# Four weight sums of a Winograd product: two by adding transfers and two on VectorE instead of four on GpSimd, with another product order

## The chip, the core and the metric

One of the eight cores of a Trainium2 chip runs the whole kernel. It has five engines with a queue of instructions each, which are synchronised by semaphores: TensorE (PE in the profile) multiplies, VectorE (DVE), ScalarE (ACT) and GpSimd (POOL) work element by element, SyncE (SP) starts transfers. GpSimd can start transfers too, and only its transfers may add to what lies at the destination. The metric is the device time of one execution in microseconds, less is better: 1863.03 us is the median of three runs of the kernel before (1861.79 to 1863.89).

## The reference, cut to what matters

The reference is two transformer blocks in a row on x of 512 tokens by 1024 features, in float32. The first block has two attentions and a feed-forward layer. The second has a feed-forward layer, a mixer of two attentions, and again a feed-forward layer. These last two layers are where the change lies:

```python
def swiglu(h, w1, w3, w2):
    return (jax.nn.silu(h @ w1) * (h @ w3)) @ w2

h = modulate(x, norm_g[l, 0], mod[:, 0, 0], mod[:, 0, 1])
x = x + 0.5 * mod[:, 0, 2][:, None, :] * swiglu(h, ffn1_w1[l], ffn1_w3[l], ffn1_w2[l])
```

The inputs w1 and w3 are 1024 by 2816 each, w2 is 2816 by 1024. The change also moves the computation of the rotary angles of the second block, `rope_tables(positions, ...)`: cosines and sines for the mixer that follows the first of these layers.

## The kernel before, in words

**Layout.** Activations are kept transposed, features on the 128 partitions and the 512 tokens along the row. A float32 product is done as three: every operand is split into a high part (rounded to fp32r, by ScalarE) and a low part (the rest, by VectorE), and TensorE multiplies high by high, high by low and low by high (L1438 to L1440 for 256 columns, L1451 to L1453 and L726 to L728 for 512). Weights come from memory in chunks of 128 by 1024 (512 KB) into RAW (three buffers); ScalarE makes HI from it, VectorE makes LO = RAW - HI (L2153).

**A layer by pairs.** `ffn_by_pairs` (f = 1 and 2, at about 793 and 1548 us) treats the hidden features in tiles of 128, 22 of them. The first four tiles are made plainly. The other 18 are made by pairs: pair p even is two gate tiles, pair p odd the up tiles of the same two hidden tiles. The weights of a pair are seen as a 2 by 2 block matrix: A11 and A12 (first tile, first and second half of the features) and A21 and A22 (second tile). The tokens are cut in two halves, EARLY and LATE. Winograd's form of Strassen's scheme then needs seven products instead of eight. Besides A11, A12 and A22 it multiplies four weight sums, S1 = A21 + A22, S2 = S1 - A11, S4 = A12 - S2 and S3 = A11 - A21, with token halves or sums of token halves (TH, TL; T3 and T4 are sums of their own). Each product is 12 matmuls of 256 columns (4 blocks of features, 3 split products). There are 18 pairs and so 126 products in a layer.

**Where the sums are made.** GpSimd's `sums_of` (L643 to L662) makes the four sums with tensor_tensor into SB, each after the low part of the same sum of the pair before has been made from the same place. SyncE loads the two weight tiles of a pair into SRAW[p % 3] (L595), two transfers of 512 KB, when the pair three before has been used up.

**Order of the products.** `_products` (L72) writes the order out: S1, S2, S4, A11 of the next pair, S3, A12 of the next pair, A22. Two neighbours share a chunk buffer (HI, LO); where TOGETHER holds, both halves are split by one instruction of 1024 columns, else by two of 512. `product` (L1401) lists what TensorE waits for: the low half of the weight form, and the copies or additions that free or complete a PSUM bank. A22 waits for c22_made (L1428), S4 for p5_copied (L1424).

**The loops.** TensorE, ScalarE and VectorE each walk the same list of products s. ScalarE and VectorE first finish product s - 1 (`after_product`), then split the form of product s + 4 (`ahead_hi`, `ahead_lo`), then do what was put off (`later`). VectorE adds PSUM banks to the copies (P1C, P5C, UC), multiplies the activated gate (G) by the up values (H), and makes the low part of a hidden tile (L3009). A layer has three parts a, b and c (PARTS): 30, 56 and 40 products, each followed by a down stage (`down_blocks`, L1443) in which the hidden tiles of the part are multiplied by w2 in eight blocks of 21 or 24 matmuls, into two PSUM banks in turn, and VectorE adds each block to X (L3137). At the end of parts a and b TensorE waits for the low part of the last but one hidden tile, and before the last tile of the first block for the last. In part c it does a stretch of the down product before and after the last product A22.

**Angles.** In the down stage of part c of layer f = 1 VectorE computes the rotary angles (`angles`, L2312) before the additions to X of blocks 0 and 2, and ScalarE the tables (`table`, L1759).

## Time and profile before

| what | value |
|---|---|
| median of three runs | 1863.03 us |
| the profiled execution | 1862.07 us |
| its span, first to last instruction | 1860.3 us |
| TensorE matmul busy | 1837.5 us, 99% |
| VectorE busy | 1334.8 us, 72% |
| ScalarE busy | 857.3 us, 46% |
| GpSimd busy | 270.8 us, 15% |
| mean granted TensorE clock | 0.998 |
| bytes moved, mean | 208.25 MB, 112 GB/s |

Busy time is the union of an engine's instructions, so a busy TensorE can still lose time: matmuls overlap, and a wait shorter than the overlap does not show as idle time. The span is 1.8 us shorter than the profiled execution. Rows of a timeline have the start in us, the duration in us, the engine, the line, the operation, the output and inputs, and in brackets the idle time of the engine before it with what ended it.

### The profile page before, as it was taken

What the parts mean: (1) busy time and instruction counts of PE and PEld (TensorE: products, weight loads), DVE (VectorE), ACT (ScalarE), POOL (GpSimd) and SP (SyncE); (2) the same over time, 40 slices, a digit from 0 to 9 for tenths busy, and PEclk for the clock granted to TensorE, in tenths of its full rate; (3) what the DMA queues carried; (4) which work ended last, traced back from release to release, by engine and by line L of the source; (5) the groups of instructions that cost most, each with busy time, mean ns of one, the idle gap of its engine ahead of it and who ended that gap; (6) DMA issues with size and microseconds to landing.
All of it is one profiled execution on the core that took longest, in us unless ns stands there. A gap on an engine that the chain in (4) does not pass through costs nothing.

```text
span 1860.3 us, 27681 instructions
## 1 busy us (share of the span) xinstructions
PE 1837.5 (99%) x10112; PEld 1530.2 (82%) x10112; DVE 1334.8 (72%) x2105; ACT 857.3 (46%) x1545; POOL 270.8 (15%) x248
## 2 busy tenths in 40 slices
PE   9999999999999999999999989999999999999999
PEld 7777778888888888798988968757767889899897
DVE  7778456757766666896985886866785788689394
ACT  6465445433232233452643554446655455355262
POOL 0001000001111000151532310100000103154140
PEclk9999999999999999999999999999999999999999
DMA  5211113346666563423332122211111422322213
GB/s 187 91 57 68 60 67 115 136 135 235 227 224 224 183 213 106 159 79 110 114 107 84 49 91 91 82 64 50 47 57 69 159 95 78 135 91 103 85 52 102
DMA packets 58325, 208.25 MB, mean 112 GB/s; under 512 B 6688, under 2 KB 6816, under 8 KB 58208
## 3 DMA queue, kind: packets, MB, share of 16 engines
q1 hardware_dynamic: 47232, 167.67, 26.0%
q0 software_dynamic: 10976, 39.00, 6.4%
q8 instruction: 75, 1.23, 0.3%
q14 instruction: 42, 0.34, 0.1%
HBM read 204.48 MB, written 2.10 MB: 111 GB/s over the span
## 4 chain that ended last, share of the span: by engine, by line
PE 79%; DVE 14%; issue 5%; ACT 1%; DMA 0%; SPq 0%; DVEq 0%; ACTq 0%
PE PS L726 16%; PE PS L728 15%; PE PS L727 15%; DVE LO L2962 5%; PE PS L1451 4%; PE PS L1452 4%; PE PS L1453 4%; PE PS L1223 2%; PE PS L1438 2%; PE PS L1440 2%; PE PS L1439 2%; PE PS L1263 2%; PE PS L1250 1%; DVE LO L2153 1%; DVE HL L3009 1%
## 5 line engine op out<-in xcount | busy, mean ns | idle before, releaser
L1542 ACT ACTIVATE HI<-RAW 128x1024 fp32r<-128x1024 f32 x237 | 250.5, 1058 | 326.9 <-PE PS L728 206.6
L2153 DVE TENSOR_TENSOR LO<-RAW,HI 128x1024 fp32r<-128x1024 f32 x237 | 290.7, 1227 | 131.1 <-ACT HI L1542 129.7
L726 PE MATMUL PS<-XH,HI 128*128 128x512 f32 x848 | 337.9, 398 | 0.0
L728 PE MATMUL PS<-XH,LO 128*128 128x512 f32 x848 | 330.8, 390 | 0.0
L727 PE MATMUL PS<-XL,HI 128*128 128x512 f32 x848 | 330.4, 390 | 0.0
L726 PEld LDWEIGHTS PS<-XH,HI 128*128 128x128 f32 x848 | 159.2, 188 | 39.2 <-issue 7.8
L728 PEld LDWEIGHTS PS<-XH,LO 128*128 128x128 f32 x848 | 159.2, 188 | 34.4
L727 PEld LDWEIGHTS PS<-XL,HI 128*128 128x128 f32 x848 | 159.4, 188 | 31.0
L1438 PE MATMUL PS<-TH,HI 128*128 128x256 f32 x576 | 163.8, 284 | 5.0 <-DVE Y L3037 5.0
L1439 PE MATMUL PS<-TL,HI 128*128 128x256 f32 x576 | 163.0, 283 | 0.0
L1440 PE MATMUL PS<-TH,LO 128*128 128x256 f32 x576 | 162.9, 283 | 0.0
L1451 PE MATMUL PS<-HH,HI 128*128 128x512 f32 x352 | 138.5, 393 | 5.4 <-DVE X L3137 3.7
L1452 PE MATMUL PS<-HL,HI 128*128 128x512 f32 x352 | 137.6, 391 | 0.0
L1453 PE MATMUL PS<-HH,LO 128*128 128x512 f32 x352 | 137.5, 391 | 0.0
L650 POOL TENSOR_TENSOR SB<-SRAW 128x512 f32<-128x512 f32 x36 | 48.2, 1338 | 604.0 <-DVE LO L2956 287.8
L2962 DVE TENSOR_TENSOR LO<-SRAW,HI 128x512 fp32r<-128x512 f32 x104 | 125.2, 1214 | 12.8 <-ACT HI L1644 12.8
L1438 PE MATMUL PS<-XH,HI 128*128 128x256 f32 x432 | 122.8, 284 | 1.8 <-ACT RB L1671 1.8
L1439 PE MATMUL PS<-XL,HI 128*128 128x256 f32 x432 | 122.2, 283 | 0.0
L1440 PE MATMUL PS<-XH,LO 128*128 128x256 f32 x432 | 122.2, 283 | 0.0
L1438 PEld LDWEIGHTS PS<-TH,HI 128*128 128x128 f32 x576 | 110.4, 192 | 7.2 <-DVE LO L2956 4.2
L1439 PEld LDWEIGHTS PS<-TL,HI 128*128 128x128 f32 x576 | 110.5, 192 | 0.2
L1440 PEld LDWEIGHTS PS<-TH,LO 128*128 128x128 f32 x576 | 110.5, 192 | 0.0
(478 smaller groups left out, 3853.3 us busy)
## 6 DMA issues: line engine op xcount, KB each, us to landing
RAW<-weights SPq DMA_DIRECT2D x237, 512.0 KB, 3.5
ADA<-ada POOLq DMA_DIRECT2D x72, 512.0 KB, 4.5
SRAW<-weights SPq DMA_DIRECT2D x72, 512.0 KB, 4.3
y_out<-X SPq DMA_DIRECT2D x8, 256.0 KB, 2.0
X<-x_in SPq DMA_DIRECT2D x3, 512.0 KB, 7.6
RAW<-weights SPq DMA_DIRECT2D x4, 256.0 KB, 5.5
X<-x_in SPq DMA_DIRECT2D x2, 256.0 KB, 4.5
COND<-condition POOLq DMA_DIRECT2D x1, 512.0 KB, 4.6
```

Source lines behind the costliest of these rows:

```text
L726: mm(bank, a, moving[0][:, t, :], start=start, stop=False)
L727: mm(bank, a, moving[1][:, t, :], start=False, stop=False)
L728: ins = mm(bank, z, moving[0][:, t, :], start=False, stop=stop)
L1438: mm(bank, a, xh[:, t, :], start=opens and t == 0, stop=False, skip_group_check=True)
L1439: mm(bank, a, xl[:, t, :], start=False, stop=False, skip_group_check=True)
L1440: ins = mm(bank, z, xh[:, t, :], start=False, stop=t == 3, skip_group_check=True)
L1451: mm(bank, a, hid_high(t), start=t == own[0], stop=False)
L1452: mm(bank, a, hid_low(t), start=False, stop=False)
L1453: ins = mm(bank, z, hid_high(t), start=False, stop=t == own[-1])
L1542: A(HI[n0 % 3][:], RAW[n0 % 3][:], ACT.Copy).then_inc(sem("hi_ready"), 1)
L2153: V.tensor_tensor(LO[n0 % 3][:], RAW[n0 % 3][:], HI[n0 % 3][:].bitcast(F32), ALU.subtract)\
L2962: V.tensor_tensor(half_of(LO[n % 3], h), form(kind, p), half_of(HI[n % 3], h).bitcast(F32), ALU.subtract).then_inc(sem("lo_ready" if h els ...
```

## The change

The order of products becomes S2, S1, A11 of the next pair, S3, S4, A12 of the next pair, A22. The sums have other signs: S2 = S1 + A11, S4 = S2 + A12, S3 = A21 + A11, so every sum is an addition. The missing signs go to the token forms 1, 2 and 4 (scale -1.0 in the copy and in the subtraction that makes the low part), to the silu of the second gate tile and to the products with the second up tile.

GpSimd adds nothing itself. For each pair it starts three transfers of 256 KB: A21 from memory to one of two slots in SB, A22 from memory added to A21 in SRAW, which makes S1 in place, and A11 from memory added to the slot, which makes S3. VectorE makes S2 and S4, in the iterations of S1 and S4 of the pair before. S3 and S4 share a chunk where they are neighbours; they lie side by side in SB for odd pairs. SyncE's load of a pair waits for S4 in place of S3, and its second half also for the low part of S1.

VectorE and ScalarE put their work for the hidden tiles elsewhere in their queues: the product of the first hidden tile is one instruction of 512 columns after S4, its low part is made six products after S4, the quarters of the second tile are multiplied after A22, and its low part six products later. What is left at the end of a part is done after the last product. The angles move to the down stage of part b of layer f = 1, blocks 1 and 4, and the tables one block later in part c, from buffers of their own (ANGLE). Some semaphores are merged.

```diff
@@ -73,8 +73,8 @@
-        order += [("S1", p), ("S2", p), ("S4", p)]
-        order += [("A11", p + 1)] * (p + 1 < NPAIRS) + [("S3", p)]
+        order += [("S2", p), ("S1", p)]
+        order += [("A11", p + 1)] * (p + 1 < NPAIRS) + [("S3", p), ("S4", p)]
@@ -88,7 +88,7 @@
-            PRODUCTS[2 * v][0] + PRODUCTS[2 * v + 1][0] in ("S1S2", "S2S4") for v in range(NV)]
+            PRODUCTS[2 * v][0] + PRODUCTS[2 * v + 1][0] == "S3S4" for v in range(NV)]
@@ -590,8 +601,10 @@
-                    sp.wait_ge(*form_made(f, "S3", p - 3))
+                    sp.wait_ge(*form_made(f, "S4", p - 3))
...
+                    if m:
+                        sp.wait_ge(*low_made(f, "S1", p - 3))
@@ -642,24 +655,21 @@
             def sums_of(f, p):
...
-                w = SRAW[p % 3]
-                a11, a12, a21, a22 = w[:, 0, 0:S], w[:, 0, S:2 * S], w[:, 1, 0:S], w[:, 1, S:2 * S]
+                first, second = wst[real_pair(f, p, 0)], wst[real_pair(f, p, 1)]
+                if p > 1:
+                    pool.wait_ge(*low_made(f, "S3", p - 2))
+                elif f == 2:
+                    pool.wait_ge(sem("branch_scaled"), 2 * DT)
+                else:
+                    pool.wait_ge(sem("chunk_used"), FIRST["down1"] + 3 * DT)
+                if of_pair(f, p) > 1:
+                    pool.wait_ge(sem("s3_landed"), 32 * of_pair(f, p) - 32)
+                    pool.wait_ge(sem("s1_landed"), 16 * of_pair(f, p) - 16)
+                pool.dma_start(third_sum(p), second[:, 0:S]).then_inc(sem("s3_landed"), 16)
...
-                if p:
-                    pool.wait_ge(*low_made(f, "S1", p - 1))
-                pool.tensor_tensor(SB[:, 0, :], a21, a22, ALU.add).then_inc(sem("s_made"), 1)
-                pool.wait_ge(*raw_pair(f, p, 0))
-                if p:
-                    pool.wait_ge(*low_made(f, "S2", p - 1))
-                pool.wait_ge(*form_made(f, "S1", p))
-                pool.tensor_tensor(SB[:, 1, :], SB[:, 0, :], a11, ALU.subtract).then_inc(sem("s_made"), 1)
-                if p:
-                    pool.wait_ge(*low_made(f, "S4", p - 1))
-                pool.wait_ge(*form_made(f, "S2", p))
-                pool.tensor_tensor(SB[:, 2, :], a12, SB[:, 1, :], ALU.subtract).then_inc(sem("s_made"), 1)
-                if p:
-                    pool.wait_ge(*low_made(f, "S3", p - 1))
-                pool.tensor_tensor(SB[:, 3, :], a11, a21, ALU.subtract).then_inc(sem("s_made"), 1)
+                pool.dma_start(SRAW[p % 3][:, 1, 0:S], second[:, S:2 * S], accum_op=ALU.add).then_inc(sem("s1_landed"), 16)
+                pool.wait_ge(sem("s3_landed"), 32 * of_pair(f, p) - 16)
+                pool.dma_start(third_sum(p), first[:, 0:S], accum_op=ALU.add).then_inc(sem("s3_landed"), 16)
@@ -1409,7 +1419,7 @@
                     elif kind == "A11" and p > 1 and p % 2 == 0:
...
                     elif kind == "A11" and p > 1:
-                        pe.wait_ge(sem("hid"), hid_count(f, pair_tile(p - 2, 1)))
+                        pe.wait_ge(sem("h21_made"), NPAIRS // 2 * (f - 1) + p // 2)
@@ -1676,23 +1687,32 @@
-                    A(G[1][:, EARLY], bank, ACT.Silu).then_inc(sem("part_silu"), 1)
+                    A(G[1][:, EARLY], bank, ACT.Silu, scale=-1.0).then_inc(sem("part_silu"), 1)
...
+            def silu_of_first(f, s):
...
+            def high_of_second(f, s):
+                kind, p = PRODUCTS[s]
+                if p % 2 and kind == "A22":
+                    hidden_hi(f, pair_tile(p, 1), H[1])
@@ -1722,13 +1742,18 @@
+                        if s > 2 * v0 + 3:
+                            silu_of_first(f, s - 4)
+                            high_of_second(f, s - 4)
...
-                    later(f, 2 * v1 - 1)
+                    for s in range(2 * v1 - 4, 2 * v1):
+                        silu_of_first(f, s)
+                        high_of_second(f, s)
@@ -1741,7 +1766,8 @@
-                            if m in (0, 2):
+                            if m in (1, 3):
+                                act.wait_ge(sem("hid_lo"), FT * f + FT)
@@ -3017,39 +3045,77 @@
                 if kind == "A12":
                     v.wait_ge(*product_done(f, kind, p))
...
+                    if p % 2:
+                        v.wait_ge(sem("hid_lo"), split_count(f, pair_tile(p - 2, 0)))
+                    elif p:
+                        v.wait_ge(sem("hid"), hid_count(f, pair_tile(p - 1, 0)))
...
-                    if p % 2:
-                        v.wait_ge(sem("c11_made"), of_pair(f, p))
-                        v.wait_ge(sem("part_silu"), part_silu(f, p, 1))
-                        V.tensor_tensor(H[0][:, EARLY], H[0][:, EARLY], G[0][:, EARLY], ALU.mult)
                 elif kind == "S4":
                     v.wait_ge(*product_done(f, kind, p))
...
-                        v.wait_ge(sem("part_silu"), part_silu(f, p, 2))
-                        V.tensor_tensor(H[0][:, LATE], H[0][:, LATE], G[0][:, LATE], ALU.mult)\
-                            .then_inc(sem("hid"), 1)
+                        v.wait_ge(sem("part_silu"), part_silu(f, p, 3))
+                        V.tensor_tensor(H[0], H[0], G[0], ALU.mult).then_inc(sem("hid"), 1)
                 elif kind == "S3":
                     v.wait_ge(*product_done(f, kind, p))
...
+                    if p % 2 == 0 and p:
+                        v.wait_ge(sem("hid"), hid_count(f, pair_tile(p - 1, 1)))
+                    elif p:
+                        v.wait_ge(sem("hid_lo"), split_count(f, pair_tile(p - 2, 1)))
...
-                    if p % 2:
-                        v.wait_ge(sem("c22_made"), of_pair(f, p))
-                        v.wait_ge(sem("part_silu"), part_silu(f, p, 3))
-                        V.tensor_tensor(H[1][:, LATE], H[1][:, LATE], G[1][:, LATE], ALU.mult)
                 elif kind == "A22" and p % 2:
                     v.wait_ge(*product_done(f, kind, p))
...
-                    V.tensor_tensor(H[1][:, EARLY], G[1][:, EARLY], bank, ALU.mult).then_inc(sem("hid"), 1)
-            def later(f, s):
+                    V.scalar_tensor_tensor(out=H[1][:, EARLY], in0=bank, scalar=-1.0, in1=G[1][:, EARLY],
+                                           op0=ALU.mult, op1=ALU.mult).then_inc(sem("h21_made"), 1)
+            def second_sum(f, p):
+                if p:
+                    v.wait_ge(*low_made(f, "S2", p - 1))
+                elif f == 2:
+                    v.wait_ge(sem("branch_scaled"), 2 * DT)
+                v.wait_ge(*form_made(f, "S1", p))
+                v.wait_ge(*raw_pair(f, p, 0))
+                V.tensor_tensor(form("S2", p), form("S1", p), form("A11", p), ALU.add).then_inc(sem("s_made"), 1)
+            def fourth_sum(f, p):
+                if p:
+                    v.wait_ge(*low_made(f, "S4", p - 1))
+                v.wait_ge(*form_made(f, "S2", p))
+                V.tensor_tensor(form("S4", p), form("S2", p), form("A12", p), ALU.add).then_inc(sem("s_made"), 1)
+            def sums_for(f, s):
...
-                if p % 2 and kind in ("S4", "A22"):
-                    m = int(kind == "A22")
-                    hidden_lo(f, pair_tile(p, m), H[m])
+                if kind == "S1" and p + 1 < NPAIRS:
+                    second_sum(f, p + 1)
+                elif kind == "S4" and p + 1 < NPAIRS:
+                    fourth_sum(f, p + 1)
+            def last_quarter(f, s):
+                kind, p = PRODUCTS[s]
+                if kind == "A22" and p % 2:
+                    v.wait_ge(sem("c22_made"), of_pair(f, p))
+                    V.scalar_tensor_tensor(out=H[1][:, LATE], in0=H[1][:, LATE], scalar=-1.0, in1=G[1][:, LATE],
+                                           op0=ALU.mult, op1=ALU.mult).then_inc(sem("hid"), 1)
+            def low_of_first(f, s):
+                kind, p = PRODUCTS[s]
+                if p % 2 and kind == "S4":
+                    hidden_lo(f, pair_tile(p, 0), H[0])
+            def low_of_second(f, s):
+                kind, p = PRODUCTS[s]
+                if p % 2 and kind == "A22":
+                    hidden_lo(f, pair_tile(p, 1), H[1])
@@ -3085,21 +3150,24 @@
+                second_sum(f, 0)
...
+                fourth_sum(f, 0)
...
                     for s in range(2 * v0, 2 * v1):
...
-                            if PRODUCTS[s - 1][0] == "S3":
-                                ahead_lo(v_chunk(f, (s - 1) // 2), ((s - 1) % 2,))
-                        if PRODUCTS[s][0] != "S3":
-                            ahead_lo(v_chunk(f, s // 2), (s % 2,))
-                        if s > 2 * v0 + 2:
-                            later(f, s - 3)
+                        ahead_lo(v_chunk(f, s // 2), (s % 2,))
+                        sums_for(f, s)
+                        if s > 2 * v0 + 1:
+                            last_quarter(f, s - 2)
+                        if s > 2 * v0 + 5:
+                            low_of_first(f, s - 6)
+                            low_of_second(f, s - 6)
@@ -3108,8 +3176,10 @@
-                    for s in range(2 * v1 - 3, 2 * v1):
-                        later(f, s)
+                    last_quarter(f, 2 * v1 - 1)
+                    for s in range(2 * v1 - 6, 2 * v1):
+                        low_of_first(f, s)
+                        low_of_second(f, s)
@@ -3119,12 +3189,11 @@
-                        if squares and m == 0:
+                        if part == 1 and f == 1 and m == 0:
...
-                            angles(2, POS2[:], "freq_a")
-                        if squares and m == 2:
-                            angles(3, POS2[:], "freq_i")
+                        if part == 1 and f == 1 and m in (1, 4):
+                            angles(2 + m // 4, POS2[:], ("freq_a", "freq_i")[m // 4])
```

## Rows read from the trace of the kernel before

**Rows 1.** The page: the chain that ended last, share of the span by engine.
```profile
PE 79%; DVE 14%; issue 5%; ACT 1%; DMA 0%; SPq 0%; DVEq 0%; ACTq 0%
```
**Rows 2.** Timeline of TensorE around 938 us: a wait between two products.
```profile
937.27 0.28 PE L1440 MATMUL PS<-XH,LO 128*128 128x256 f32 x1
938.00 0.36 PE L1438 MATMUL PS<-TH,HI 128*128 128x256 f32 x1 [0.46 <-DVE Y L3037]
938.20 0.28 PE L1439 MATMUL PS<-TL,HI 128*128 128x256 f32 x1
938.32 0.28 PE L1440 MATMUL PS<-TH,LO 128*128 128x256 f32 x1
```
**Rows 3.** Busy time by stretch: PE, PEld, DVE, ACT, POOL, clock, DMA, GB/s.
```profile
917.87:939.17 21.30, 20.61 (x171) 20.26 (x170) 20.91 (x25) 12.30 (x24) 11.50 (x9) 1.00 0.28 96
```
**Rows 4.** Waits of TensorE, 795 to 1062 us: total, times, longest.
```profile
PE PS L1438 <- DVE Y L3037: 2.5, 5, 0.9
PE PS L1438 <- ACT RB L1671: 0.9, 4, 0.2
```
**Rows 5.** Groups of GpSimd, 917.87 to 939.17 us: total and mean ns, idle before.
```profile
L650 POOL TENSOR_TENSOR SB<-SRAW 128x512 f32<-128x512 f32 x2 | 2.6, 1294 | 4.8 <-DVE LO L2956 2.6 <-DVE LO L2962 2.2
```
**Rows 6.** Groups of VectorE in the same stretch.
```profile
L2962 DVE TENSOR_TENSOR LO<-SRAW,HI 128x512 fp32r<-128x512 f32 x6 | 7.7, 1298 | 0.3 <-ACT HI L1644 0.3
L2962 DVE TENSOR_TENSOR LO<-SB,HI 128x512 fp32r<-128x512 f32 x4 | 3.8, 961 | 0.0
```
**Rows 7.** Timeline of VectorE in a down stage, GpSimd idle.
```profile
873.90 0.68 DVE L2962 TENSOR_TENSOR LO<-SB,HI 128x512 fp32r<-128x512 f32 x1
874.50 0.68 DVE L2962 TENSOR_TENSOR LO<-SRAW,HI 128x512 fp32r<-128x512 f32 x1
```
**Rows 8.** GpSimd's ADA transfers (L640), and VectorE's use of them (L2336), min/median/max.
```profile
DMA to landing us min/median/max: 3.6/4.5/7.2
L2336 DVE SCALAR_TENSOR_TENSOR ADA<-ADA,COND x72: 1210/1218/1227, 354.8 to 707.8; 128x1024 f32<-128x1024 f32 x72
```
**Rows 9.** Timeline of TensorE and VectorE at the end of part a.
```profile
838.79 0.28 PE L1440 MATMUL PS<-TH,LO 128*128 128x256 f32 x1
839.51 0.50 PE L1451 MATMUL PS<-HH,HI 128*128 128x512 f32 x1 [0.44 <-DVE HL L3009]
...
838.77 0.68 DVE L3009 TENSOR_TENSOR HL<-Y,HH 128x512 fp32r<-128x512 f32 x1
839.37 0.41 DVE L3020 TENSOR_TENSOR SQ<-RB,PS 128x256 f32<-128x256 f32 x1
```
**Rows 10.** Timeline of VectorE, down stage of part c: subtraction, angles, X.
```profile
1069.60 1.23 DVE L2153 TENSOR_TENSOR LO<-RAW,HI 128x1024 fp32r<-128x1024 f32 x1
1070.74 0.42 DVE L3124 CAST POS<-POS 128x512 f32<-128x512 int32 x1
...
1075.17 0.74 DVE L3137 SCALAR_TENSOR_TENSOR X<-PS,MOD,X 128x512 f32<-128x512 f32 x1
```
**Rows 11.** Timeline of TensorE in the same stage.
```profile
1072.93 0.39 PE L1453 MATMUL PS<-HH,LO 128*128 128x512 f32 x1
1075.97 0.79 PE L1451 MATMUL PS<-HH,HI 128*128 128x512 f32 x1 [2.64 <-DVE X L3137]
...
1088.39 0.50 PE L1451 MATMUL PS<-HH,HI 128*128 128x512 f32 x1 [1.03 <-DVE X L3137]
```
**Rows 12.** Two more gaps of TensorE, and stretches behind gaps (columns of rows 3).
```profile
748.07 0.69 PE L800 MATMUL PS<-SQC,RB 128*128 128x1 f32 x5 [1.20 <-DVE RB L2195]
...
1111.81 1.02 PE L800 MATMUL PS<-SQC,RB 128*128 128x1 f32 x8 [1.68 <-DVE RB L2195]
...
748.00:752.00 4.00, 3.93 (x25) 3.56 (x26) 2.26 (x8) 1.44 (x4) 0.41 (x1) 1.00 0.86 315
1076.00:1079.40 3.40, 3.40 (x8) 2.72 (x9) 1.23 (x2) 3.37 (x6) 0.00 (x0) 0.50 0.00 0
1113.50:1116.90 3.40, 3.15 (x10) 2.17 (x9) 3.32 (x3) 0.67 (x2) 1.45 (x1) 0.50 0.00 0
```

More of the change, by code:

```diff
@@ L331, in form @@
         def form(kind, p):
-            if kind in S_SLOT:
-                return SB[:, S_SLOT[kind], :]
+            if kind in ("S2", "S4"):
+                return SB[:, 0 if kind == "S2" else 3, :]
+            if kind == "S3":
+                return third_sum(p)
+            if kind == "S1":
+                return SRAW[p % 3][:, 1, 0:S]
             return SRAW[p % 3][:, kind == "A22", {"A11": 0, "A12": S, "A22": S}[kind]:{"A11": S, "A12": 2 * S, "A22": 2 * S}[kind]]
@@ L345, in form_made @@
         def form_made(f, kind, p):
-            if kind in S_SLOT:
-                return sem("s_made"), 4 * (NPAIRS * (f - 1) + p) + S_SLOT[kind] + 1
+            if kind in ("S2", "S4"):
+                return sem("s_made"), 2 * (NPAIRS * (f - 1) + p) + (1 if kind == "S2" else 2)
+            if kind == "S1":
+                return sem("s1_landed"), 16 * of_pair(f, p)
+            if kind == "S3":
+                return sem("s3_landed"), 32 * of_pair(f, p)
             return raw_pair(f, p, int(kind == "A22"))
@@ L1630, in token_hi @@
                 act.wait_ge(sem("dve_tokens"), token(f, f"sum{n}"))
-                A(TH[:, n - 1], src, ACT.Copy).then_inc(sem("high_tokens"), 1)
+                A(TH[:, n - 1], src, ACT.Copy, scale=1.0 if n == 3 else -1.0).then_inc(sem("high_tokens"), 1)
             def forms_hi(f, v, halves=(0, 1)):
@@ L1637, in forms_hi @@
                 if TOGETHER[v] and 0 in halves:
-                    act.wait_ge(*form_made(f, *PRODUCTS[2 * v + 1]))
+                    for kind, p in PRODUCTS[2 * v:2 * v + 2]:
+                        act.wait_ge(*form_made(f, kind, p))
                     A(HI[n % 3][:], both_forms(v), ACT.Copy).then_inc(sem("hi_ready"), 1)
@@ L1678, in after_product @@
                     act.wait_ge(*product_done(f, kind, p))
-                    A(G[1][:, EARLY], bank, ACT.Silu).then_inc(sem("part_silu"), 1)
+                    A(G[1][:, EARLY], bank, ACT.Silu, scale=-1.0).then_inc(sem("part_silu"), 1)
             def later(f, s):
+                kind, p = PRODUCTS[s]
+                if p % 2 == 0 and kind == "S4":
+                    act.wait_ge(sem("c12_made"), of_pair(f, p))
+                    A(G[0][:, LATE], G[0][:, LATE], ACT.Silu).then_inc(sem("part_silu"), 1)
+                elif p % 2 == 0 and kind == "S3":
+                    act.wait_ge(sem("c22_made"), of_pair(f, p))
+                    A(G[1][:, LATE], G[1][:, LATE], ACT.Silu, scale=-1.0).then_inc(sem("part_silu"), 1)
+                elif p % 2 and kind == "S4":
+                    hidden_hi(f, pair_tile(p, 0), H[0])
+            def silu_of_first(f, s):
                 kind, p = PRODUCTS[s]
@@ L1686, in later @@
                     A(G[0][:, EARLY], G[0][:, EARLY], ACT.Silu).then_inc(sem("part_silu"), 1)
-                elif p % 2 == 0 and kind == "S4":
-                    act.wait_ge(sem("c12_made"), of_pair(f, p))
-                    A(G[0][:, LATE], G[0][:, LATE], ACT.Silu).then_inc(sem("part_silu"), 1)
-                elif p % 2 == 0 and kind == "S3":
-                    act.wait_ge(sem("c22_made"), of_pair(f, p))
-                    A(G[1][:, LATE], G[1][:, LATE], ACT.Silu).then_inc(sem("part_silu"), 1)
-                elif p % 2 and kind in ("S4", "A22"):
-                    m = int(kind == "A22")
-                    hidden_hi(f, pair_tile(p, m), H[m])
+            def high_of_second(f, s):
+                kind, p = PRODUCTS[s]
+                if p % 2 and kind == "A22":
+                    hidden_hi(f, pair_tile(p, 1), H[1])
             def whole_silu(f, t, bank, dst):
```

31 lines of the change are left out of this document (17 added, 14 removed).

## The prediction

> **What bounds the kernel now.** I read the chain of waits first: 79% of it is TensorE and 14% VectorE [rows 1]. So TensorE is the bound, and only the places where it waits can be won. The reader then sees in TensorE's timeline how a weight product runs when nothing waits: its matmuls of 256 columns start 0.12 us apart [rows 2], so twelve take 1.44 us, seven products (one pair) 10.08 us, and the fourteen of a gate pair and an up pair 20.16 us. The period measured is 21.30 us [rows 3]: 1.14 us per two pairs is waiting. The waits list of the first of the two layers in pairs (L1387) gives 2.5 us in five waits for VectorE's L3037 and 0.9 us in four for ScalarE's L1671; the list of the second layer has the same two lines with the same numbers [rows 4]. A wait costs more than its gap: 937.27 to 938.00 is 0.73 us between starts where 0.12 is due, 0.61 lost for a gap of 0.46, and the next start is late by another 0.07 or 0.08 [rows 2]. That is 0.23 us over the gap, so a layer loses 3.4 + 9 x 0.23 = 5.5 us, with one loss too short to be listed 5.6, and both layers **11.2 us**.
>
> Why VectorE is late: GpSimd's four sums of a pair take 1.3 us each where nothing stretches them [rows 5], and beside them VectorE's subtraction of a half weight tile takes 1.30 us where it reads SRAW and 0.96 where it reads SB [rows 6]. While GpSimd is idle both take 0.68, and the next starts after 0.60 [rows 7]. So the two engines take turns wherever VectorE reads two SBUF operands. Counted so for two pairs: ten half subtractions x 0.60, two whole ones x 1.14, two hidden ones x 0.60 and four products of halves x 0.41 (the starts of rows 7, 10 and 9) are 11.1 us, GpSimd's eight sums x 1.3 are 10.4, together 21.5, against 21.3 measured. The pair stage is tied to this turn-taking, and TensorE is tied at its ends.
>
> **The change, part by part.** *Sums.* GpSimd's 10.4 us per two pairs go. VectorE gets four additions x 0.60 = 2.4 us. Its list becomes: twelve half subtractions and one whole 8.3, sums 2.4, two hidden ones 1.2, six additions from PSUM x 0.45 (0.41 and a short wait each) = 2.7, one whole product 0.6 and two halves with a sign 0.9: 16.1 us of 20.16, with nothing beside them. The additions cannot be below 0.60 (the form is that of rows 7); the upper end is the disturbed 1.30, if transfers disturb as GpSimd did, and then all sixteen such operations cost 0.7 more, +11 us. I take 0.60: beside the 72 ADA transfers that GpSimd issued, 72 VectorE operations with two whole SBUF operands took 1.21 to 1.23 us each [rows 8], and a whole subtraction with nothing beside it took 1.23 [rows 10]. Signs cost nothing: they are scale operands of copies and of operations that were there.
>
> *Product order.* A22 now follows S3 with two products between, S4 and A12, instead of A12 alone, so VectorE has 2.88 us and not 1.44 for c22_made (L1428); S4 has two between it and S1, instead of S2 alone, for p5_copied (L1424). These are exactly the two waits of [rows 4]. What is tightest next: A11 of an odd pair needs h21_made, two products behind (2.88 us against a semaphore delay of 0.33 and 0.41 us of work), and the low halves, made four products ahead (5.76 us). In the fullest iteration (A12) VectorE has 2.3 us to do in 1.44; the neighbours have 1.0 to 1.7, so it is behind by under 1.5 us and catches up. I take the whole 11.2 us as won; ends 0 and 11.2.
>
> *Transfers.* Three per pair on GpSimd's queue, 256 KB each: S3's first term, A22 added into SRAW (S1), A11 added into S3. No row shows an adding transfer. Nearest are GpSimd's plain ones: ADA of 512 KB lands in 3.6 to 7.2 us, median 4.5 [rows 8]. These are the two ends for a write and for an addition, and I take the median for each, and for SyncE's load of SRAW. S1: with t the end of A22 of pair p-3, the buffer is free four products earlier, the load lands by about t - 1.8, GpSimd issues by about t + 0.2 and it lands at t + 4.7; VectorE wants it eight products behind t, at t + 11.5. That is 6.8 us of cover. The throughput is the nearer limit: GpSimd waits for the previous pair's last addition before it starts (the two s3_landed waits), so a pair costs it a write and an addition in series, 4.5 + 4.5 = 9.0 us of 10.08. SyncE's queue is not moved: its pair loads also wait for S1's low half, which is made before A22's. The DMA engines are busy for 28% [rows 3] and get 0.75 MB on top of 1 MB per pair, under half.
>
> The Trainium skill, "DMA: Bandwidth & Descriptors" (section Anatomy of one DMA), fits a GpSimd-issued transfer with 2.0 us plus bytes over 436 GB/s, 2.6 us for 256 KB: an estimate of 5.2 us a pair instead of 9.0. By either the sum is the same; no row here shows the form that adds.
>
> *Ends of parts a and b.* Here something is lost. With t the start of A22's last matmul, 838.79, the down product starts at 839.51 now, and waits for the low half of the first hidden tile (838.77) [rows 9]. After the change that low half stands behind two operations of A22's tile, since `low_of_first(f, s-6)` falls past the part's end: VectorE sees A22 about 0.33 us after t, needs 0.41 for each of the two quarters, a short wait between them, and 0.68 for the low half: t + 1.8. TensorE loses 1.7 instead of 0.6 us: 1.1 x 4 ends = **+4.4 us**. Bounds: 0 (if the low half slips in ahead) and 4.4 plus the clock, below. Part c is covered: TensorE works 3.4 us on early tiles after A22.
>
> *Angles.* They leave the last down stage of the first pair layer. There they hold VectorE from 1070.74 to 1075.17, when X's addition begins [rows 10], and TensorE starts 2.81 us late at 1075.97 (3.04 us between starts, 0.23 due). At half clock its next eight matmuls lose 1.7 us (3.4 us at 0.50), and it waits 1.03 again at 1088.39, 1.3 us in all [rows 11, 12]. Without them X is done by about 1072.9 and the third block is due at 1073.2. **-5.8 us**. In part b's down stage they go between a subtraction and X: 1.2 + 0.7 + 4.0 = 5.9 us of VectorE in a block of 5.5 us (24 matmuls x 0.23), but two PSUM banks alternate, so X may be a block late, and the other blocks leave 3.6 us. The two table calls move one block later on ScalarE, whose next split is wanted 8 us on. Cost 0; at worst a repeat of the 1.0 wait, twice.
>
> *Opening.* second_sum and fourth_sum of the first pair add 1.2 us to VectorE ahead of the first products. TensorE has no wait there in either layer, and the first loss comes in the second pair, so I take 0; the other end is 1.2 in each layer.
>
> **Sum.** -11.2 + 4.4 - 5.8 = -12.6 us. The profiled execution took 1862.07 us for a span of 1860.3; it becomes 1849.5. The runs shown have a median of 1863.03, 1 us above it, so 1850.4.
>
> **Rivals.** *Transfers pace the pairs (slower).* If write plus addition passes 10.08 us, every pair beyond those fetched ahead (some 12 of 18 in a layer) is late by the excess. With 4.5 and 7.2 it is 1.6 us x 24 = 39, less 12.6: 1889. It decides from an addition of 5.6 us on; at an excess of 0.5 us, an addition of 6.1, the gain is gone. For it: 7.2 us occurs [rows 8]. Against: half the bytes. Chance 0.11.
>
> *The clock falls at the longer waits.* The granted clock was 0.50, 1.2 GHz, after gaps of 2.64 and 1.68 us and stayed 1.00, 2.4 GHz, after one of 1.20 [rows 11, 12]; a fall cost 1.7. My new waits are in between, at a gap of about 1.55. Four falls: +6.8, 1857.2. [...] Chance 0.13.
>
> *VectorE's queue takes over.* Its in-order waits for landings and for the hid counts put back the losses in the products: 11.2 not won, 4.4 - 5.8 = -1.4, 1861.6. For it: six new waits. Against: 4 us of slack per two pairs. Chance 0.10.
>
> *The slow subtraction is not GpSimd's doing* but the place read (SRAW 1.30, SB 0.96). Then VectorE, busy for 20.91 us of 21.30 now [rows 3], has 2.4 more, 23.3 us: 2 us x 18 slower, 1899, the other terms left out. [Rows 7] speak against it. Chance 0.02. That the sums do not leave GpSimd is excluded by the diff.
>
> *The ends of the parts cost nothing*: 1846. Chance 0.06.
>
> **How the numbers follow.** The forecast has 0.58, its own range 1846 to 1855. The range 1845 to 1862 takes in the clock rival and most of the third, and leaves out the transfers. A measurement here can tell 0.2%, 3.7 us: under 1859.3 is faster: 0.58 + 0.06 + 0.12 and a little of the third, 0.78; within 0.09; slower 0.13.
>
> **What would show it.** Half subtractions at 0.68 throughout; no GpSimd sums; the period of two pairs 20.2 us; no wait for c22_made or L1671; gaps of about 1.5 us before the down products of parts a and b, released by the low half; no gap near 1073 to 1088; adding transfers landing in under 5.6 us. Wrong, if SRAW landings release VectorE or the period stays at 21.3.

## The result, and the profile after

| | before | after |
|---|---|---|
| median, lowest to highest | 1863.46 us (1861.79 to 1863.95), four runs | 1849.58 us (1848.17 to 1851.60), four runs |
| profiled execution, its span | 1862.07, 1860.3 us | 1850.16, 1848.4 us |

The ratio of after to before is 0.9924, 95% interval 0.9909 to 0.9938: faster by 13.9 us, where 12.6 were forecast. Rows of after are read here as those of before were. First the page of the changed kernel, the chain that ended last (share of the span by engine):

```profile
PE 94%; DVE 3%; issue 1%; ACT 1%; DMA 0%; SPq 0%; DVEq 0%; ACTq 0%
```

VectorE held 14% of the chain in [rows 1] and holds 3% now. Those are shares of a chain and not time that can be won: 11% of the span is some 200 us, and 13.9 were won. The stretch of two pairs that answers to [rows 3], the same columns:

```profile
916.62:936.78 20.16, 20.16 (x170) 20.16 (x170) 15.95 (x29) 12.51 (x26) 4.64 (x6) 1.00 0.71 181
```

The two pairs take 20.16 us, fourteen products of twelve matmuls at 0.12 us, and TensorE waits for nothing. VectorE is busy for 15.95 us instead of 20.91. The DMA share went from 0.28 to 0.71 and the rate from 96 to 181 GB/s. VectorE's groups in that stretch, against [rows 6] (total and mean ns, idle time before):

```profile
L2989 DVE TENSOR_TENSOR LO<-SRAW,HI 128x512 fp32r<-128x512 f32 x8 | 5.5, 688 | 2.5 <-ACT HI L1655 2.4
L2989 DVE TENSOR_TENSOR LO<-SB,HI 128x512 fp32r<-128x512 f32 x4 | 2.8, 690 | 1.6 <-ACT HI L1655 1.6
L3083 DVE TENSOR_TENSOR SB<-SRAW 128x512 f32<-128x512 f32 x2 | 1.4, 686 | 0.0
```

Both kinds of half subtraction take 0.69 us, where they took 1.30 and 0.96, and so do the additions that came to VectorE. The transfers do not slow it. TensorE's waits from 792 to 1110 us, the first layer in pairs, against [rows 4]:

```profile
PE PS L1461 <- DVE HL L3037: 3.3, 2, 1.6
PE PS L810 <- DVE RB L2222: 1.7, 1, 1.7
PE PS L832 <- DVE RB L2248: 0.9, 1, 0.9
PE PS L761 <- DVE RB L2820: 0.3, 1, 0.3
```

The two waits of [rows 4] are gone, and so is that of X in the down stages ([rows 11], L3137 there, L3206 now). What is left is the norm behind the layer (the last three lines; before, they were 1.7, 0.2 and 0.3 us) and, twice, the wait for the low half of a hidden tile at the ends of parts a and b, which was 0.44 us in [rows 9] and is the one that grew. TensorE and VectorE around the first of them, against [rows 9]:

```profile
837.78 0.28 PE L1450 MATMUL PS<-TH,LO 128*128 128x256 f32 x1
839.71 0.50 PE L1461 MATMUL PS<-HH,HI 128*128 128x512 f32 x1 [1.65 <-DVE HL L3037]
...
836.84 1.22 DVE L2180 TENSOR_TENSOR LO<-RAW,HI 128x1024 fp32r<-128x1024 f32 x1
837.97 0.41 DVE L3052 TENSOR_TENSOR SQ<-RB,PS 128x256 f32<-128x256 f32 x1
838.30 0.42 DVE L3072 SCALAR_TENSOR_TENSOR Y<-PS,SQ 128x256 f32<-128x256 f32 x1
838.64 0.41 DVE L3105 SCALAR_TENSOR_TENSOR Y<-Y,SQ 128x256 f32<-128x256 f32 x1
838.97 1.47 DVE L3037 TENSOR_TENSOR HL<-Y,HH 128x512 fp32r<-128x512 f32 x2
```

1.93 us between two starts where 0.12 is due: 1.81 lost for a gap of 1.65. ScalarE's high half of the first tile was ready at 837.6; VectorE came to its low half (L3037) only behind the second tile's quarters.

Where the 11.9 us between the spans came from, each loss measured between starts, as the prediction did it:

| place | before | after | difference | forecast |
|---|---|---|---|---|
| products of both layers, waits and late starts within a product | 11.3 | 0.0 | -11.3 | -11.2 |
| four ends of parts a and b | 2.8 | 7.7 | +4.9 | +4.4 |
| down stage of part c, f = 1 (two waits and the half clock) | 5.8 | 0 | -5.8 | -5.8 |
| sum | | | -12.2 | -12.6 |

Both executions have one more stretch of 3.41 us at half clock, beside a norm: at 1113.5 us before ([rows 12]) and at 751.4 after. They nearly cancel. The changed kernel comes to its first pairs 1.2 us later than the kernel before, and behind the later norm the kernel before has lost 0.9 us more; what is left of the two is the 0.3 us between -12.2 and -11.9.

Not every two pairs of the kernel before take the 21.30 us of [rows 3]. Part b has four times two pairs. The first two of them ran without a wait of TensorE, the last two at 21.30 us. This is the stretch just ahead of [rows 3]:

```profile
897.71:917.87 20.16, 20.16 (x169) 20.03 (x168) 19.77 (x24) 12.18 (x24) 10.36 (x9) 1.00 0.26 98
```

Its half subtractions are as slow as those of [rows 6] (1.30 and 0.96 us) and GpSimd adds as much, yet TensorE loses nothing. The reading that fits is that VectorE starts a part ahead of TensorE and falls back by about 1.1 us with every two pairs, and TensorE waits only when that lead is gone; the lead itself was not measured. The prediction's 11.2 us do not depend on it, since they were summed from the waits and not from 21.30 us times the number of pairs.

### The profile page after: what moved, and what is told of

It is laid out like the page before. It is cut to its first block, busy times and chain, and to the rows that moved or that the text cites. A ratio compares the mean times of both kernels' runs of the same rounds, so it can differ in the third digit from the quotient of the medians.

```text
span 1848.4 us, 27707 instructions
## 1 busy us (share of the span) xinstructions
PE 1830.8 (99%) x10112; PEld 1528.3 (83%) x10112; DVE 1269.8 (69%) x2179; ACT 861.5 (47%) x1565; POOL 143.4 (8%) x212
## 4 chain that ended last, share of the span: by engine, by line
PE 94%; DVE 3%; issue 1%; ACT 1%; DMA 0%; SPq 0%; DVEq 0%; ACTq 0%
PE PS L736 16%; PE PS L738 15%; PE PS L737 15%; PE PS L1450 6%; PE PS L1449 6%; PE PS L1448 6%; PE PS L1461 4%; PE PS L1463 4%; PE PS L1462 4%; PE PS L1233 2%; PE PS L1273 2%; PE PS L1260 1%; PE PS L844 1%; PE PS L845 1%; PE PS L848 1%
## 5 line engine op out<-in xcount | busy, mean ns | idle before, releaser
L2989 DVE TENSOR_TENSOR LO<-SRAW,HI 128x512 fp32r<-128x512 f32 x140 | 96.4, 688 | 42.5 <-ACT HI L1655 39.5
L3206 DVE SCALAR_TENSOR_TENSOR X<-PS,MOD,X 128x512 f32<-128x512 f32 (+1 forms) x49 | 36.1, 739 | 100.6 <-PE PS L1463 100.6
```

The costliest lines, as they stand in the source:

```text
L2989: V.tensor_tensor(half_of(LO[n % 3], h), form(kind, p), half_of(HI[n % 3], h).bitcast(F32), ALU.subtract).then_inc(sem("lo_ready" if h els ...
```

## The experiments

Each was timed beside the kernel before on the same chip; the ratio is to that one. What is given as over or under the changed kernel is against its 1849.58 us, unless c1 is named. x4, x5 and x6 have two runs each, so their medians are rough.

**The old kernel without GpSimd's work** (y1). GpSimd adds one column instead of 512 in each of its four sums, and S1, S3 and the others are read where A22 lies. The weight sums are thus left out.

```diff
-                pool.tensor_tensor(SB[:, 0, :], a21, a22, ALU.add).then_inc(sem("s_made"), 1)
+                pool.tensor_tensor(SB[:, 0, 0:1], a21, a22, ALU.add).then_inc(sem("s_made"), 1)
...
-                return SB[:, S_SLOT[kind], :]
+                return SRAW[p % 3][:, 1, 0:S]
```

> The kernel before with its product order, but GpSimd's four sums are cut to one column each, so that nothing stands beside VectorE; the four sums are left out of the computation and the products take half of the raw tile instead. Theory (turn-taking of GpSimd and VectorE is the whole loss in the products): the period of two pairs falls from 21.30 to about 20.2 us although the order is the old one, 11.2 us are won, 1852. Rival (the old order with 1.44 us before A22 is the loss): the waits for c22_made stay, the period stays above 20.9 and the time above 1858.

Measured: 1849.96 us (1848.91 to 1851.59), ratio 0.9929, interval 0.9913 to 0.9946. Two pairs and VectorE's group of that stretch:

```profile
910.00:930.16 20.16, 20.16 (x171) 20.16 (x170) 13.89 (x25) 12.18 (x25) 2.09 (x8) 1.00 0.29 105
```
```profile
L2962 DVE TENSOR_TENSOR LO<-SRAW,HI 128x512 fp32r<-128x512 f32 x10 | 6.9, 689 | 4.3 <-ACT HI L1644 4.3
```

The old order, with nothing beside VectorE, loses nothing in the products either: 20.16 us, and the read of SRAW takes 0.69. So the products' 11.3 us go when GpSimd's additions go, whatever the order, and the place read is no cause. The four ends lose 1.9 us here instead of 2.8. This run alone can't tell whether the additions hurt by slowing VectorE or by coming late to it; in [rows 6] VectorE is idle for 0.3 us in its subtractions and busy for 20.91 of 21.30 [rows 3], which speaks for the first, and x5 below tests it.

**The new order with GpSimd's sums** (y2). The changed kernel, with all four sums, as additions, on GpSimd.

```diff
-                pool.dma_start(third_sum(p), second[:, 0:S]).then_inc(sem("s3_landed"), 16)
...
+                pool.tensor_tensor(third_sum(p), a21, a11, ALU.add).then_inc(sem("s3_landed"), 1)
+                pool.wait_ge(*form_made(f, "S3", p))
+                pool.tensor_tensor(a21, a21, a22, ALU.add).then_inc(sem("s1_landed"), 1)
```

> The changed kernel with its order, but all four sums are made by GpSimd as before (S3, then S1 in place, S2, S4), no adding transfers, no sums on VectorE. Theory (turn-taking): 11.1 + 10.4 us of exclusive work do not fit in 20.16, the period goes back to 21.2 to 21.5 us and the 11.3 us of the products come back: about 1861. Rival (the order makes the difference): period 20.2 us, the time within 2 us of the changed kernel's 1849.6.

Measured: 1856.95 us (1856.05 to 1858.48), ratio 0.9964, interval 0.9951 to 0.9976. Between the two theories. Two pairs late in part b, GpSimd's and VectorE's costliest groups, and the wait that is left:

```profile
929.14:949.91 20.77, 20.38 (x168) 20.20 (x169) 19.55 (x25) 12.29 (x26) 13.11 (x9) 1.00 0.28 101
```
```profile
L670 POOL TENSOR_TENSOR SB<-SRAW 128x512 f32<-128x512 f32 x3 | 4.9, 1627 | 1.4 <-DVE LO L2991 1.3
```
```profile
L2991 DVE TENSOR_TENSOR LO<-SRAW,HI 128x512 fp32r<-128x512 f32 x9 | 9.8, 1092 | 0.8 <-ACT HI L1657 0.7
```
```profile
PE PS L1450 <- DVE SQ L3070: 1.8, 4, 0.7
```

The two engines still stretch each other (1.63 us on GpSimd, 1.09 on VectorE), but the layers lose 6.1 us in the products instead of 11.3. The wait that is left is that of A22 for c22_made (L3070), although two products now stand before it; that of S4 for p5_copied is gone. So the rest of the change, without the new places of the sums, wins about half. That is the order, and with it VectorE's new list: this run doesn't part the two. The expectation took 11.1 us for VectorE from the old list. By the prediction's own prices y2's list (twelve half subtractions, one whole, two hidden low halves, one product of 512 columns and one of 256 with both operands in SBUF) is 10.6 us, an estimate, and with GpSimd's 10.4 it makes 21.0, against 20.77 measured.

**The angles back** (y3), in the changed kernel, and **the angles moved alone** (b1), in the kernel before.

```diff
-                        if part == 1 and f == 1 and m == 0:
+                        if squares and m == 0:
...
-                        if part == 1 and f == 1 and m in (1, 4):
-                            angles(2 + m // 4, POS2[:], ("freq_a", "freq_i")[m // 4])
+                            angles(2, POS2[:], "freq_a")
+                        if squares and m == 2:
+                            angles(3, POS2[:], "freq_i")
```

> The changed kernel with the angles back in the down stage of part c of the first pair layer (blocks 0 and 2) and the tables back with them. Theory: TensorE waits again for X, some 2.8 and 1.0 us, and if the clock falls 1.7 more: +3.9 to +5.8 us over the changed kernel, 1853.5 to 1855.4. Rival (VectorE has more room now and hides them): within 1 us of 1849.6.

> The kernel before with only the angles and tables moved as in the change. Theory: -5.8 us, 1857.7, and no gap of TensorE in the down stages of parts b and c beside those at their starts. Rival (part b's down stage has no room): a new wait of about 1 us or more in part b and a gain under 4 us.

Measured: y3 1855.91 us (1855.79 to 1857.46), ratio 0.9962 (0.9948 to 0.9976), 6.3 over the changed kernel. b1 1858.04 us (1855.66 to 1861.27), ratio 0.9964 (0.9950 to 0.9978), 5.7 under the kernel before beside it. TensorE in y3, the only idle times in the down stage of part c:

```profile
1073.65 0.50 PE L1461 MATMUL PS<-HH,HI 128*128 128x512 f32 x1 [2.98 <-DVE X L3207]
...
1086.14 0.50 PE L1461 MATMUL PS<-HH,HI 128*128 128x512 f32 x1 [1.06 <-DVE X L3207]
```

After the first of them the granted clock was 0.50 for 3.4 us, as before the change. In b1 there are none, nor in part b's stage, and its product waits are those of [rows 4] (2.6 and 0.9 us). The angles are worth 5.7 to 6.3 us from either side, and their new place costs nothing.

**Plain transfers** (x6). The two transfers that add write only, in the same places, so the sums S1 and S3 are left out.

```diff
-                pool.dma_start(SRAW[p % 3][:, 1, 0:S], second[:, S:2 * S], accum_op=ALU.add).then_inc(sem("s1_landed"), 16)
+                pool.dma_start(SRAW[p % 3][:, 1, 0:S], second[:, S:2 * S]).then_inc(sem("s1_landed"), 16)
...
-                pool.dma_start(third_sum(p), first[:, 0:S], accum_op=ALU.add).then_inc(sem("s3_landed"), 16)
+                pool.dma_start(third_sum(p), first[:, 0:S]).then_inc(sem("s3_landed"), 16)
```

> The changed kernel with plain transfers in place of the two adding ones, so S1 and S3 are not the right sums. Theory: TensorE's time is the same within 1 us (the landings are covered), the transfers land in about 3 us instead of 4.5 and 5.9, and the busy share of the DMA engines in the pair stage falls from 0.71 to about 0.4. Rival (adding itself is not what is dear, the number of transfers is): landings and share stay as they are.

Measured: 1848.68 us (1848.56 to 1848.80), ratio 0.9926 (0.9906 to 0.9946): the changed kernel's time. Its stretch of two pairs:

```profile
916.62:936.78 20.16, 20.16 (x170) 20.16 (x169) 15.96 (x29) 12.51 (x26) 3.21 (x7) 1.00 0.56 183
```

Time from the issue of a transfer to its landing, least, median and most, of the write, of S1's and of S3's transfer (L668, L670, L672), first in the changed kernel:

```profile
DMA to landing us min/median/max: 2.8/3.0/6.9
DMA to landing us min/median/max: 4.0/4.5/6.5
DMA to landing us min/median/max: 3.7/5.9/8.8
```

and here:

```profile
DMA to landing us min/median/max: 2.8/3.0/5.4
DMA to landing us min/median/max: 3.0/3.1/6.3
DMA to landing us min/median/max: 2.8/3.5/6.2
```

So the adding costs 1.4 to 2.4 us a transfer at the median, none of which reaches TensorE (20.16 us either way), and 0.15 of DMA share (0.71 against 0.56) at the same rate.

**One more addition** (x4). A11 is added into S3 a second time, in series. S3 is then not the sum that the reference needs.

```diff
-                pool.wait_ge(sem("s3_landed"), 32 * of_pair(f, p) - 16)
+                pool.wait_ge(sem("s3_landed"), 48 * of_pair(f, p) - 32)
+                pool.dma_start(third_sum(p), first[:, 0:S], accum_op=ALU.add).then_inc(sem("s3_landed"), 16)
+                pool.wait_ge(sem("s3_landed"), 48 * of_pair(f, p) - 16)
                 pool.dma_start(third_sum(p), first[:, 0:S], accum_op=ALU.add).then_inc(sem("s3_landed"), 16)
```

> The changed kernel with the addition of A11 into the slot of S3 done twice, one after the other, so S3 is not the right sum. The measured landings are 3.0 for the write and 5.9 for the addition, so a pair costs GpSimd's queue some 15 us instead of 9. Theory (series of transfers against 10.08 us a pair decides): TensorE waits for sums in the parts, some 4.7 us for each of about 12 pairs a layer that are not fetched ahead: +80 to +130 us, about 1950. Rival (transfers overlap or there is enough lookahead): under +10 us.

Measured: 1884.17 us (1881.36 to 1886.99), ratio 1.0116 (1.0096 to 1.0137). GpSimd's start of each pair's first transfer, first in the changed kernel, where the landing of the last addition released it:

```profile
919.84 0.57 POOL L668 DMA_DIRECT2D SB<-weights  x1 [5.55 <-DMA SB<-weights]
930.56 0.57 POOL L668 DMA_DIRECT2D SB<-weights  x1 [6.64 <-DMA SB<-weights]
939.98 0.57 POOL L668 DMA_DIRECT2D SB<-weights  x1 [5.21 <-DMA SB<-weights]
```

then with one more addition (the profile shows no releaser for these), what ScalarE waits for from 880 to 965 us, and what it makes of TensorE:

```profile
919.60 0.57 POOL L668 DMA_DIRECT2D SB<-weights  x1 [4.18 <-issue]
933.15 0.57 POOL L668 DMA_DIRECT2D SB<-weights  x1 [5.09 <-issue]
947.86 0.57 POOL L668 DMA_DIRECT2D SB<-weights  x1 [6.44 <-issue]
```
```profile
ACT HI L1657 <- DMA SB<-weights: 8.7, 2, 6.9
```
```profile
949.23 0.35 PE L1450 MATMUL PS<-XH,HI 128*128 128x256 f32 x1 [3.99 <-DVE Y L3074]
962.03 0.36 PE L1450 MATMUL PS<-XH,HI 128*128 128x256 f32 x1 [1.01 <-ACT SQ L1692]
```

A pair costs the queue 13.6 to 14.7 us instead of 10.08, ScalarE waits for landings, and TensorE behind it, so the rival of the transfers is a real mechanism. It cost 34.6 us over the changed kernel (its two runs are 5.6 apart) and not the 100 expected. The trace tells where: the products lose 24.4 us, of which 20.6 in the two parts b, 3.5 in the parts c and 0.3 in the parts a, whose pairs are fetched ahead. The ends with their down stages lose 8.5 more. Five stretches of 3.4 us at half clock are in this; each came with a gap of 2.64 to 3.99 us. In the changed kernel the queue is close to that point: 10.72 and 9.42 us for two pairs running, with TensorE's 10.08 between them. It isn't past it: the previous addition's landing released only 15 of its 36 pairs, and VectorE, which frees the slot, 19.

**VectorE's two sums three times over** (x5).

```diff
+                for _ in range(2):
+                    link(V.tensor_tensor(form("S2", p), form("S1", p), form("A11", p), ALU.add))
                 V.tensor_tensor(form("S2", p), form("S1", p), form("A11", p), ALU.add).then_inc(sem("s_made"), 1)
...
+                for _ in range(2):
+                    link(V.tensor_tensor(form("S4", p), form("S2", p), form("A12", p), ALU.add))
                 V.tensor_tensor(form("S4", p), form("S2", p), form("A12", p), ALU.add).then_inc(sem("s_made"), 1)
```

> VectorE makes each of its two sums of a pair three times over, the same result written to the same place. VectorE's work for two pairs goes from 15.95 us to about 20.8 us, TensorE's stays at 20.16 us. Theory (the later of the two engines paces the pairs, losses add up over 18 double pairs): some 0.6 us for each of 18 double pairs and about 1 us more at each of six ends of parts, 1862 to 1870 us. Rival (three buffers deep and lookahead into the down stages take it up): under 4 us, 1849 to 1853 us. It measures how much of VectorE's slack the change leaves is real.

Measured: 1883.15 us (1881.89 to 1884.40), ratio 1.0104 (1.0086 to 1.0123): 31.9 over the changed kernel beside it (c1, 1851.29), far outside both. Two pairs, and the end of part a with the stretch behind it:

```profile
929.73:951.13 21.40, 20.44 (x169) 20.26 (x169) 20.94 (x37) 11.84 (x26) 4.51 (x6) 1.00 0.71 175
...
845.80:849.10 3.30, 3.30 (x9) 2.52 (x9) 2.38 (x3) 0.71 (x1) 0.00 (x0) 0.50 0.45 150
```
```profile
845.56 0.68 PE L1461 MATMUL PS<-HH,HI 128*128 128x512 f32 x1 [4.10 <-DVE HL L3037]
```

Nothing but VectorE's list was made longer here, and with VectorE busy for 20.94 us two pairs take 21.40, nearly the 20.91 and 21.30 of [rows 3]. That is the test that y1 could not make: a list of that length is enough to hold TensorE, whatever GpSimd does. As before the change, part b loses this only in the last two of its four times two pairs.

The products lose 16.0 us in both layers, where 11 were expected. The other half is at the four ends of parts a and b and in the down stages behind them, 17.9 us. VectorE comes to these ends with a backlog: the gap grows from 1.65 to 4.10 us and the loss between starts from 1.81 to 4.26, 9.8 us more in all. The remaining 8.1 us are the clock: beside every one of these gaps the granted clock was 0.50 for 3.4 or 6.8 us, 20.5 us in all. With 0.4 us elsewhere this makes the 34.3 us between the spans of the two profiled executions (1882.7 and 1848.4).

**The low part early** (e1), then **the sum late too** (e2). At an end of part a or b, the low half of the first tile is made before the last product is finished. e2 also puts the fourth sum of the next pair, which stood ahead of it, behind that product.

```diff
+                        if part < 2 and s == 2 * v1 - 2:
+                            low_of_first(f, s - 1)
...
-                        sums_for(f, s)
+                        if part == 2 or s != 2 * v1 - 3:
+                            sums_for(f, s)
...
+                    if part < 2:
+                        sums_for(f, 2 * v1 - 3)
...
-                        low_of_first(f, s)
+                        if part == 2 or s != 2 * v1 - 3:
+                            low_of_first(f, s)
```

> The changed kernel, but at the ends of parts a and b VectorE makes the low part of the first hidden tile right after its product with the gate, ahead of the split of the next down chunk, and not behind the last product. Theory: ScalarE's high part is ready 0.2 us before A22's last matmul starts, the low part is made 0.6 us after it, and TensorE loses 0.5 to 0.6 us instead of 1.81 plus 0.11: 4 x 1.3 = 5.2 us faster than the changed kernel, 1844.4. Rival (the wait moves to the last hidden tile or to the delayed down chunk): under 2 us.

> As e1, and the fourth sum of the next pair, which stands between the end of S4 and the work on its bank, is put off to behind the last product of the part. Theory: the whole chain of the first tile starts 0.5 us earlier, the low part is there when TensorE wants it: 4 x 1.9 = 7.5 us faster than the changed kernel, 1842. Rival: no better than e1, because ScalarE or the down chunk ends the wait.

Measured: e1 1847.14 us (1842.34 to 1848.59), ratio 0.9909 (0.9892 to 0.9925); e2 1844.37 us (1843.71 to 1846.76), ratio 0.9906 (0.9890 to 0.9923). By the trace e1 leaves 0.47 us of 1.81 at each of the four ends, and e2 none. That is 5.4 us for e1, as expected, but its median is only 2.4 under the changed kernel's: its profiled execution has 13.7 us at half clock beside the two norms, against 3.4 in the changed kernel's. The intervals overlap that of the changed kernel, so the changed kernel (c1) and e2 (e3) were run again side by side.

> The changed kernel once more, beside the kernel with the low part early and the sum late, on one chip with the same runs of the kernel before. Expected of the clock: if the falls of the granted clock around the norms come by chance, the median lies within 2 us of 1849.6, and the profiled execution may show another number of half-clock stretches than the first one did. Rival: the single half-clock stretch at 751 us belongs to the new order; then it is there again.

> The same program as e2_low_early_sum_late. Theory: at four ends of parts it saves the 1.81 and 0.11 us that the changed kernel loses there, 7.7 us by the trace, so against the changed kernel in this call it is 5 to 8 us faster (1842 to 1845 us). Rival: the 5.2 us between the two medians so far are half noise of the clock falls; then it comes out 2 to 4 us faster only (1846 to 1848 us).

Measured: c1 1851.29 us (1848.83 to 1852.19, five runs), ratio 0.9930 (0.9917 to 0.9944); e3 1843.14 us (1841.59 to 1846.28, four runs), ratio 0.9892 (0.9877 to 0.9907). TensorE and VectorE in e3:

```profile
838.78 0.28 PE L1450 MATMUL PS<-TH,LO 128*128 128x256 f32 x1
838.90 0.41 PE L1461 MATMUL PS<-HH,HI 128*128 128x512 f32 x1
...
838.07 0.69 DVE L3037 TENSOR_TENSOR HL<-Y,HH 128x512 fp32r<-128x512 f32 x1 [0.70 <-ACT HH L1667]
```

The down product follows the last weight product after 0.12 us. Side by side the gain is 8.2 us, where the trace gives 7.7, and the intervals are apart. This version beats both kernels.

## Why the prediction was right, and where not

*Products, -11.2: right in size and in cause, rough in its model.* Both waits that it named are gone, and the losses measured are 11.3. Two causes were treated as one, though. Taking GpSimd's additions away is enough by itself (y1), and the order with VectorE's new list wins half without it (y2); the change does both, so what they win does not add up. Whether the order is needed with VectorE's own sums in place of GpSimd's was not run. The sum by strict turns came near both times (21.5 for 21.3, and 21.0 for 20.77 in y2), but it gives the pace of VectorE's list, not that of every pair: half of part b ran at 20.16 before the change as well.

*VectorE's list, 16.1 us of 20.16: right.* 15.95 measured. x5 shows where the slack of 4.2 us ends: with 5.0 us more the period is 21.40, of which VectorE is busy for 20.94 and waits for 0.46. So the rival that its queue takes over did not come in the parts; it came, in small, at their ends.

*Ends of parts, +4.4: mechanism right, 0.5 us too small.* 1.81 us and not 1.7 for each, against 0.59 and not 0.6 before, and 0.11 us more in the next start, before and after alike. The cause is that VectorE takes the first tile's low half behind the second tile's quarters, as e1 shows by moving it: 1.34 of the 1.81 go. The other 0.47 was the fourth sum, which stood ahead in the same queue (e2).

*Angles, -5.8: right*, from both sides (y3, b1).

*Opening, 0: right.* No product of either layer starts late.

*Transfers: the conclusion was right, its sizes were not, and luck had a part.* S3's addition lands in 5.9 us at the median, over the 5.6 at which the rival was to decide. That it didn't is owed to the write, which took 3.0 instead of 4.5. Two errors nearly cancel: write and addition in series take 8.9 us by the medians and 9.4 to 10.7 in the pairs shown, instead of 9.0. The estimate by the Trainium skill, "DMA: Bandwidth & Descriptors" (section Anatomy of one DMA), 2.6 us for 256 KB, is near the plain write (3.0) and far below the adding form (4.5 and 5.9). The DMA engines were to be busy for under half; they are busy for 0.71. The bytes were counted rightly (181 GB/s against 96), but 0.56 of the 0.71 is what those bytes cost when they only write (x6), and [rows 3] has 0.28 for 96 GB/s: the forecast had scaled that share by the bytes of weights, 0.28 x 1.75 = 0.49. Of the miss of 0.22 the adding is 0.15; the other 0.07 was there with plain writes. The cover was thinner than it said: one more addition cost 34.6 us.

*The clock at the longer waits, 0.13: didn't come.* After the gap of 1.65 us the clock stayed at 1.00, sixteen times of sixteen (the changed kernel, c1, y3 and x6). But the reading of [rows 12] that stood behind this rival, that the length of a gap decides, holds only for the long ones. TensorE in the changed kernel:

```profile
748.10 0.58 PE L810 MATMUL PS<-SQC,RB 128*128 128x1 f32 x4 [1.21 <-DVE RB L2222]
...
751.40:754.80 3.40, 3.40 (x12) 2.74 (x11) 1.97 (x4) 0.93 (x4) 1.77 (x2) 0.50 0.59 140
```

Here the fall followed a gap of 1.21 us, where [rows 12] show none after the same gap, and none followed the 1.70 us gap at the later norm, where [rows 12] have one. Over the thirteen profiled executions a fall came beside the earlier norm nine times and beside the later one seven times: beside one of them in eight executions, beside both in four and beside neither in one. The same program fell at the earlier norm for 3.4 us in one execution and for 6.8 us in another (after and c1). At the earlier norm the layer behind it starts some 1.7 us later for 3.4 us of half clock and some 3.1 for 6.8; at the later norm it is 0.6 to 0.9 and 2.7, since TensorE's wait there is shorter when its clock is low (0.2 us before the change, 0.9 after). These come on top of any sum and can account for differences of 2 us and more between runs; that the medians lie 13.9 us apart and the terms 12.2 is within that. Why a fall comes in one execution and not in the next stays open.

## What to carry to other kernels

When work leaves an engine that shares memory with another, count what it did to that other one: here GpSimd's 11.5 us per two pairs cost VectorE 7.0 (20.91 against 13.89 in y1), and VectorE held the matmuls. A period read in one stretch need not hold for all: before the change VectorE's lead hid the loss in half of part b. Slack in the steady state is not slack at the ends: a few operations that stand in the wrong order in one queue cost 7.7 us at four ends, more than half of what the whole change won, and a backlog of 2.5 us there also cost the clock (x5). A transfer that adds is a cheap way to make a sum if its own chain of landings has room; measure the chain against the period of the consumer, and not the bytes against the share of the DMA engines.

## What the hardware showed beyond that

- A 256 KB transfer from memory into SBUF lands in 3.1 and 3.5 us (medians, x6) when it writes and in 4.5 and 5.9 when it adds (the changed kernel), and its issue holds GpSimd for 0.86 to 0.91 us instead of 0.54.
- VectorE's subtraction with two SBUF operands takes 0.69 us beside adding transfers at 0.71 DMA share, and 1.09 to 1.10 beside GpSimd's additions (y2), which themselves take 1.61 to 1.75 there and took 1.29 to 1.68 in the stretch of [rows 5].
- Of TensorE's gaps in the thirteen executions all twelve of 2.64 to 4.10 us (before, y1, y3, x4, x5) had a half clock beside them; one of 2.34 us (x4) had none, and none of the twenty-one of 1.52 to 1.69 us at ends of parts and between products (after, c1, y2, y3, x4, x6). At the norms a gap of 1.20 or 1.21 us had one in nine cases of thirteen, and one of 1.68 to 1.71 us in seven of thirteen. TensorE's matmuls there have one column (128x1, L810); whether that is the difference was not tested.
